# Seven-product down projection: unit widths, two sets of raw weights, and who adds the helping sum

## The chip, the core and the metric

The kernel runs on one core of a Trainium2 chip. Its engines run side by side, each through its own queue in order, and meet at semaphores: TensorE (PE; its weight loads are PEld), VectorE (DVE), ScalarE (ACT), GpSimd (POOL) and SyncE (SP), which here only issues DMAs. The metric is the device time of one execution in microseconds.

## The reference

Two layers of a bidirectional encoder over 1024 positions and width 1024, in float32: latent attention, then a gated MLP, differential attention, then another gated MLP, with a norm before each sub-layer and one at the end. The change touches the second half of the MLP alone:

```python
def conv_ffn(h, w_up, conv_w, conv_b, w_down):
    u = h @ w_up                       # 1024 -> 2 * 2816
    u = depthwise_conv3(u) + conv_b    # over positions
    g, val = jnp.split(u, 2, axis=-1)
    return (jax.nn.silu(g) * val) @ w_down   # 2816 -> 1024
...
    x = x + conv_ffn(rmsnorm(x, ffn_norm_g[i]), ...)
```

## The kernel before

Each float32 matmul is made of three passes over operands split in a high and a low part (`passes`): high by high, high by low, low by high. A split is a copy to the high part on ScalarE and a subtraction for the low part, on GpSimd for weights and on VectorE for activations.

Both MLP matmuls use a fast scheme with seven products instead of eight (Strassen's, in Winograd's form). For the down projection, weights and activations y are cut in 2 x 2 blocks; seven products of sums of blocks (0 to 6, in the order of `DOWN_A`: A11, S2, A12, S1, S4, S3, A22) give the four quarters of the output. S1 to S4 are sums of raw weight blocks, which GpSimd makes (`sum_a`). The sums of y blocks (T1 to T4) are made while the up projection runs, and stored in DRAM with the blocks; SP loads them back (`load_y`), and the weights (`load_a`: the even half holds A11 and A21, the odd half A12 and A22).

The inner width of 2816 is cut in 11 pairs. `SUPER` joins them in units: unit 0 is one pair wide, units 1 to 5 two. A unit runs its seven products, so there are 42 steps. One product makes four banks of PSUM (i = 0 to 3), with 12 matmuls a pair. VectorE adds each bank to a total in SBUF (`add_product`), four instructions a product. Products 0 and 1 go into `common`, a helping sum that three quarters of the output need; product 3 goes into `fifth`, which two need; 2, 4, 5 and 6 go straight into the output `x_out`, which already holds x. Products 2 and 6 continue in the banks of products 0 and 5, so product 6 waits until product 5 has been added, bank by bank. After the last `fifth` product VectorE adds `common` to `fifth` (L1363) and both to the output (L1346), between the last products' adds.

The order is that of the code. VectorE runs `low_y(step + 4)`, the split of a y block four steps ahead, before `add_product(step)`. ScalarE runs `high(g, n)` for each step in turn: the high part of the weight block, then that of the y block. GpSimd runs, for each unit, S1, S2, low A11, S4, low S2, low A12, low S1, S3, low S4, low S3, low A22; `sum_a` writes the raw sum over the low part of the unit before, so it waits for that product. There is one set of raw weights, and SP (`fetch`) asks for the next unit's even half when the sum S3 and the low parts are made.

At the start of the projection the up projection of the last pair still ends: its product with A22 (`fourth`), VectorE's `finish`, convolution and y sums. At the end ScalarE squares the output, GpSimd sums the squares (L1205, L1208) and TensorE adds over partitions (L1479), for the next norm; in layer 0 GpSimd first splits two weights of the next phase (L360).

## Time and profile before

| what | value |
|---|---|
| median of 3 runs (lowest, highest) | 2931.86 us (2930.26, 2936.58) |
| profiled execution, its span | 2930.89 us, 2929.0 us |
| busy PE, DVE, ACT, POOL | 93%, 69%, 49%, 55% |
| down projection of layer 0 (to the square sums) | 1182.3 to 1464.7 us |
| down projection of layer 1 | 2632.3 to 2908.1 us |

A row of a timeline has the start in us from the span's start, the duration, the engine, the line, the operation, what it writes and reads, and how many such instructions in a row were merged. In brackets stand the idle time before it and what ended that. Matmuls are pipelined, so that rows of PE overlap: the time from start to start is what a matmul costs. Instructions of the other engines also overlap by some 0.08 us.

### The profile page before, as it was taken

The page shows a single profiled execution, that of the slowest core. Times are in us where ns is not written, and L with a number is a line of the kernel's source. Part 1 is how long each engine was busy: PE and PEld are TensorE (multiplying, and loading weights), DVE is VectorE, ACT ScalarE, POOL GpSimd, SP SyncE. Part 2 cuts the span into 40 slices and gives each one's busy share as a digit, 9 for nine tenths or more (in the row PEclk, how much of TensorE's full clock was granted, in tenths as well). Part 3 has the DMA queues.
Part 4 walks back from the last instruction along what each step waited for, and adds up shares of the span by engine and source line. Part 5 has one row for each costly group of instructions (what it writes and reads, how often), then busy time and mean ns, then how long its engine had stood idle before and what let it go on. Part 6 is the DMA issues. An engine that isn't in the chain of part 4 may idle for free. (4 is left out here: it accounts for less than half of the span.)

```text
span 2929.0 us, 40309 instructions
## 1 busy us (share of the span) xinstructions
PE 2712.9 (93%) x13444; PEld 2274.4 (78%) x13444; DVE 2023.4 (69%) x2669; ACT 1421.3 (49%) x2182; POOL 1612.6 (55%) x1163
## 2 busy tenths in 40 slices
PE   8899999989899999699789999998898999997997
PEld 6788888878778888577678888887786888875775
DVE  6577777762766666677778888887428666667777
ACT  5577777761444444332345666665324444433332
POOL 2355554543787776576743333331237777765774
PEclk9999999999999999799999999999999999997998
DMA  3000000013132222544120010000331222225431
GB/s 134 22 11 10 7 10 7 15 64 114 36 116 106 98 99 107 201 138 137 43 110 22 30 37 29 31 20 22 151 110 43 106 94 107 107 104 204 145 130 65
DMA packets 90590, 230.00 MB, mean 79 GB/s; under 512 B 8944, under 2 KB 12272, under 8 KB 89968
## 3 DMA queue, kind: packets, MB, share of 16 engines
q1 hardware_dynamic: 90480, 228.57, 21.4%
q8 instruction: 65, 1.06, 0.1%
q14 instruction: 45, 0.37, 0.0%
HBM read 166.14 MB, written 62.39 MB: 78 GB/s over the span
## 5 line engine op out<-in xcount | busy, mean ns | idle before, releaser
L1377 PE MATMUL ffn_ps<-ffn_b_hi,weights_hi 128*128 128x512 f32 x704 | 277.8, 395 | 21.0 <-POOL weights_lo L720 12.2
L1379 PE MATMUL ffn_ps<-ffn_b_hi,weights_lo 128*128 128x512 f32 x704 | 276.7, 393 | 0.0
L1378 PE MATMUL ffn_ps<-ffn_b_lo,weights_hi 128*128 128x512 f32 x704 | 276.5, 393 | 0.0
L360 POOL TENSOR_TENSOR weights_lo<-weights_raw,weights_hi 128x1024 fp32r<-128x1024 f32 (+2 forms) x65 | 127.5, 1966 | 207.1 <-ACT weights_hi L355 207.1
L720 POOL TENSOR_TENSOR up_local_lo<-up_sums,up_local_hi 128x512 fp32r<-128x512 f32 x126 | 170.8, 1358 | 98.2 <-ACT up_local_hi L715 98.2
L2482 ACT ACTIVATE dif_p<-dif_s,dif_neg_max 128x1024 f32<-128x1024 f32 x128 | 142.2, 1114 | 121.9 <-DVE dif_neg_max L2669 115.5
L1377 PE MATMUL ffn_ps<-ffn_b_hi,up_local_hi 128*128 128x512 f32 x504 | 196.6, 390 | 0.0
L1378 PE MATMUL ffn_ps<-ffn_b_lo,up_local_hi 128*128 128x512 f32 x504 | 196.4, 390 | 0.0
L1379 PE MATMUL ffn_ps<-ffn_b_hi,up_local_lo 128*128 128x512 f32 x504 | 196.1, 389 | 0.0
L2572 POOL TENSOR_TENSOR dif_q_lo<-dif_rotated,dif_q_hi 64x512 fp32r<-64x512 f32 x64 | 85.1, 1330 | 182.5 <-ACT dif_q_hi L2464 178.8
L715 ACT ACTIVATE up_local_hi<-up_sums 128x512 fp32r<-128x512 f32 x126 | 79.0, 631 | 216.4 <-PE ffn_ps L1379 153.4
L2034 DVE TENSOR_REDUCE mat_row_max<-lat_s 128x1 f32<-128x1024 f32 x128 | 156.1, 1220 | 39.1 <-PE lat_s L371 38.1
L1887 ACT ACTIVATE mat_pt_hi<-mat_turn 128x512 fp32r<-128x512 f32 x256 | 138.9, 594 | 85.3 <-PE mat_turn L2160 85.0
L1377 PEld LDWEIGHTS ffn_ps<-ffn_b_hi,weights_hi 128*128 128x128 f32 x704 | 133.9, 190 | 52.7 <-issue 17.9
L1979 POOL TENSOR_TENSOR mat_passed<-mat_inv_sum 128x1 f32<-128x1 f32 x128 | 24.7, 193 | 264.2 <-DVE mat_inv_sum L2042 264.1
L1237 DVE SCALAR_TENSOR_TENSOR ffn_conv<-ffn_ps,vecs,ffn_conv 128x1023 f32<-128x1023 f32 x88 | 112.5, 1278 | 81.7 <-ACT ffn_conv L1035 81.7
L2669 DVE TENSOR_REDUCE dif_neg_max<-dif_s 128x1 f32<-128x1024 f32 x128 | 150.3, 1215 | 23.6 <-PE dif_s L2785 23.6
L2049 DVE TENSOR_TENSOR mat_pt_lo<-mat_turn,mat_pt_hi 128x512 fp32r<-128x512 f32 x256 | 162.8, 677 | 5.0 <-ACT mat_pt_hi L1887 5.0
L1115 ACT ACTIVATE ffn_hi_S<-ffn_raw_S 128x1024 fp32r<-128x1024 f32 (+1 forms) x48 | 47.1, 982 | 242.3 <-POOL ffn_raw_S L1176 242.3
L1907 ACT ACTIVATE mat_probs<-lat_s,mat_shift 128x1024 f32<-128x1024 f32 x128 | 143.5, 1121 | 25.6 <-DVE mat_shift L2037 25.3
L1378 PEld LDWEIGHTS ffn_ps<-ffn_b_lo,weights_hi 128*128 128x128 f32 x704 | 133.9, 190 | 27.8
L1379 PEld LDWEIGHTS ffn_ps<-ffn_b_hi,weights_lo 128*128 128x128 f32 x704 | 133.6, 190 | 28.1
(381 smaller groups left out, 8861.7 us busy)
## 6 DMA issues: line engine op xcount, KB each, us to landing
ffn_y_raw<-ffn_products SPq DMA_DIRECT2D x50, 512.0 KB, 3.5
weights_raw<-in_up SPq DMA_DIRECT2D x44, 512.0 KB, 3.3
up_raw<-in_up SPq DMA_DIRECT2D x44, 512.0 KB, 3.9
ffn_products<-ffn_y_sum SPq DMA_DIRECT2D x88, 256.0 KB, 2.2
ffn_a_raw<-in_down SPq DMA_DIRECT2D x44, 512.0 KB, 5.5
weights_raw<-in_diff_qkv SPq DMA_DIRECT2D x23, 512.0 KB, 3.2
ffn_products<-ffn_conv SPq DMA_DIRECT2D x44, 256.0 KB, 2.1
weights_raw<-ffn_products SPq DMA_DIRECT2D x20, 512.0 KB, 5.0
```

The source lines that it names most:

```text
L360: pool.tensor_tensor(w.lo[:], w.raw[:], w.hi[:].bitcast(F32), ALU.subtract).then_inc(w.lo_done, 1)
L720: pool.tensor_tensor(w.lo[name], w.block_raw(par, name), w.hi[name].bitcast(F32), ALU.subtract).then_inc(w.lo_done, 1)
L1237: dve.scalar_tensor_tensor(cv[:, 1:SEQ], pr[:, 0:SEQ - 1], vec(V_CONV_W + 2 * FT * 3 * layer, s, q), cv[:, 1:SEQ], ALU.mult, ALU.add).then ...
L1377: pe.matmul(out, hi, x_hi, start=start, stop=False, skip_group_check=True)
L1378: pe.matmul(out, hi, x_lo, start=False, stop=False, skip_group_check=True)
L1379: return pe.matmul(out, lo, x_hi, start=False, stop=stop, skip_group_check=True)
L1887: act.activation(pt[:, 4 * half:4 * half + 4, (t % 2) * P:(t % 2 + 1) * P], turn_ps[half][:].rearrange("p (k m) -> p k m", m=P), ACT.Copy) ...
L1907: act.activation(probs[t % 4][:], s_ps[t % 2][:], ACT.Exp, bias=shift[:, col:col + 1], scale=MLA_SCALE, accum_out=row_sum[:, col:col + 1]) ...
L2034: dve.tensor_reduce(row_max[:, col:col + 1], s_ps[t % 2][:], AX_X, ALU.max, negate=True).then_inc(max_ready, 1)
L2049: dve.tensor_tensor(pt_lo[b][part], turn_ps[half][:].rearrange("p (k m) -> p k m", m=P), pt_hi[b][part].bitcast(F32), ALU.subtract).then_i ...
L2482: act.activation((p0, p1)[m][t % 2][:], s_ps[m][:], ACT.Exp, bias=neg_max[:, col:col + 1], accum_out=total).then_inc(exp_done, 1)
L2669: dve.tensor_reduce(neg_max[:, col:col + 1], s_ps[m][:], AX_X, ALU.max, negate=True).then_inc(max_ready, 1)
```

## The change

The units are now (0, 1), (2, 3), ..., (8, 9), and 10 alone: the single pair stands last. There are two sets of raw weights (`even0`, `odd0`, `even1`, `odd1`), used in turn; the low part of A12, which lies on its raw block, has two places too. The raw sums S1 to S4 still have one place each. SP asks for both halves of a unit's weights first in `fetch`, and for y blocks 0 and 1 of unit 0 behind its weights, before the last stores of the up projection. `fourth` now runs between banks 1 and 2 of the first product. The adds of `common` to the output move from VectorE to GpSimd, 12 instructions in the place of VectorE's 8 (it no longer goes by way of `fifth`), and VectorE's early order changes. Both MLP layers run the same code.

```diff
 DOWN_SUMS = ("S1", "S2", "S4", "S3")
 Y_ROW = {B11: 0, T2: 1, B21: 2, T1: 3, B22: 4, T3: 5, T4: 6}
-SUPER = [(0, 1)] + [(2 * g - 1, 2) for g in range(1, 6)]
+SUPER = [(2 * g, 2) for g in range(5)] + [(10, 1)]
 STEPS = 7 * len(SUPER)
 COMMON, LAST_COMMON = (0, 1, 3), STEPS - 4
 DOWN_FINAL = [(k, 0, STEPS - 5) for k in range(4)] + [(k, 1, STEPS - 3) for k in range(4)] + \
@@ -733,7 +733,12 @@
 
 def added(step, i):
 
-    return 4 * step + i + 1 + (12 if step > LAST_COMMON else 0) + (4 if step > LAST_COMMON + 1 else 0)
+    return 4 * step + i + 1 + (4 if step > LAST_COMMON else 0) + (4 if step > LAST_COMMON + 1 else 0)
+
+
+def loaded(g):
+
+    return 16 * sum(width for first, width in SUPER[:g + 1])
 
 
 def stored(q, even):
...
-        self.a_raw = {"A11": ar[:, 0], "A21": ar[:, 1], "A12": ar[:, 2], "A22": ar[:, 3]}
+        self.even = [kb(f"even{b}", place, F32, (2, 2, 4, P)) for b, place in enumerate((124, 112))]
+        self.odd = [kb(f"odd{b}", place, F32, (2, 2, 4, P)) for b, place in enumerate((132, 176))]
+        self.a_own = [{"A11": even[:, 0], "A21": even[:, 1], "A12": odd[:, 0], "A22": odd[:, 1]}
...
@@ -948,7 +962,7 @@
 
             def load_a(g, odd):
                 first, width = SUPER[g]
-                tile, done = (down.odd, odd_loaded) if odd else (down.even, even_loaded)
+                tile, done = (down.odd[g % 2], odd_loaded) if odd else (down.even[g % 2], even_loaded)
                 for j in range(width):
                     sp.dma_start(tile[:, :, j], down_dram[2 * (first + j) + odd].rearrange("p (a k) m -> p a k m", a=2)) \
                       .then_inc(done, 16)
@@ -965,6 +979,9 @@
...
                     load_a(0, 1)
+                    sp.wait_ge(lo_done, block_no(PAIRS - 2, "A22"))
+                    load_y(0, 0)
+                    load_y(0, 1)
                 elif not (isinstance(p, int) and p == PAIRS - 2):
                     sp.wait_ge(lo_done, block_no(p, "A22"))
                     load_raw(p + 2, par)
...
 
-            sp.wait_ge(lo_done, block_no(PAIRS - 2, "A22"))
-            load_y(0, 0)
-            load_y(0, 1)
             sp.wait_ge(prod, product_no(PAIRS - 1, "P1"))
             load_y(0, 2)
             sp.wait_ge(prod, product_no(PAIRS - 1, "P6"))
...
             store_y(PAIRS - 1, False)
 
             def fetch(g):
+                if g == 1:
+                    sp.wait_ge(y_stored, 112 * GROUPS)
+                else:
+                    sp.wait_ge(a_summed, 4 * g - 4)
+                    sp.wait_ge(a_lo_done, 7 * g - 7)
+                    multiplied(sp, 7 * g - 12)
+                load_a(g, 0)
+                load_a(g, 1)
                 for n in range(2):
                     sp.wait_ge(y_lo_done, 7 * g - 7 + n + 1)
                     load_y(g, n)
-                sp.wait_ge(a_summed, 4 * g)
-                sp.wait_ge(a_lo_done, 7 * g - 6)
-                load_a(g, 0)
-                multiplied(sp, 7 * g - 5)
-                load_y(g, 2)
-                sp.wait_ge(a_lo_done, 7 * g)
-                load_a(g, 1)
-                for n in range(3, 7):
+                for n in range(2, 7):
                     multiplied(sp, 7 * g - 7 + n)
                     load_y(g, n)
 
...
             def sum_a(g, name, first, second, op, loads, sums):
-                width, raw_a = SUPER[g][1], down.a_raw
+                width = SUPER[g][1]
                 for done in loads:
-                    pool.wait_ge(done, 32 * g + 16 * width - (16 if g else 0))
+                    pool.wait_ge(done, loaded(g))
                 need(pool, a_summed, 4 * g + sums)
                 multiplied(pool, 7 * g - 7 + DOWN_A.index(name))
...
                 low_a(g, "S3")
                 low_a(g, "A22")
+            for n in (4, 5, 6):
+                for i in range(4):
+                    pool.wait_ge(acc_added, added(LAST_COMMON - 2, i))
+                    pool.tensor_tensor(x_part(n, i), x_part(n, i), down.common[:, i, :], ALU.add).then_inc(common_added, 1)
             if ahead:
                 ahead.split_low(pool)
             for n, (k, half, step) in enumerate(DOWN_FINAL[:-1]):
...
                     ins.then_inc(acc_added, 1)
 
-            def shared(n, i):
-
-                return added(LAST_COMMON, 3) + {6: 4, 4: 8, 5: 16}[n] + i + 1
-
-            def add_common(n):
+            def add_fifth(n):
                 for i in range(4):
-                    if n != 6:
-                        dve.wait_ge(acc_added, added(LAST_COMMON, 3) + i + 1)
-                    dve.tensor_tensor(x_part(n, i), x_part(n, i), (down.common if n == 6 else down.fifth)[:, i, :],
-                                      ALU.add).then_inc(acc_added, 1)
+                    dve.wait_ge(acc_added, added(LAST_COMMON, i))
+                    dve.wait_ge(common_added, 4 * (n - 4) + i + 1)
+                    dve.tensor_tensor(x_part(n, i), x_part(n, i), down.fifth[:, i, :], ALU.add).then_inc(acc_added, 1)
 
             low_y(0)
             low_y(1)
             finish(PAIRS - 1, 1)
             add_product(0)
+            low_y(2)
             finish_y(PAIRS - 1, False)
             sum_y(PAIRS - 1, False)
-            low_y(2)
             low_y(3)
+            add_product(1)
             low_y(4)
-            for step in range(1, LAST_COMMON + 1):
+            low_y(5)
+            for step in range(2, LAST_COMMON + 1):
                 low_y(step + 4)
                 add_product(step)
-            for i in range(4):
-                dve.wait_ge(acc_added, added(LAST_COMMON, i))
-                dve.tensor_tensor(down.fifth[:, i, :], down.fifth[:, i, :], down.common[:, i, :],
-                                  ALU.add).then_inc(acc_added, 1)
-            add_common(6)
-            add_common(4)
+            add_fifth(4)
             add_product(STEPS - 3)
-            add_common(5)
+            add_fifth(5)
             add_product(STEPS - 2)
             add_product(STEPS - 1)
             norm_mean(dve, out_norm)
...
                 for i in range(4):
+                    if between and i == 2:
+                        between()
                     if g == 0 and not more and i in (0, 2) and n in (0, 1):
                         if n == 0 and i == 2:
                             pe.wait_ge(u2_done, PAIRS - 1)
...
+            multiply_down(0, lambda: fourth(PAIRS - 1))
             for step in range(1, STEPS):
                 multiply_down(step)
             parts = ((out_norm.acc, 1, 0, out_norm.sq_added, 12), (out_norm.acc, 0, 0, out_norm.sq_added, 15),
```

VectorE in the last unit of layer 0, from the add of its product 2 on. Before (`ffn_ps` is PSUM, `x_first` the output):

```order
L1335 TENSOR_TENSOR x_first<-x_first,ffn_ps 128x512 x4
L1335 TENSOR_TENSOR ffn_fifth<-ffn_fifth,ffn_ps 128x512 x4
L1363 TENSOR_TENSOR ffn_fifth<-ffn_fifth,ffn_common 128x512 x4
L1346 TENSOR_TENSOR x_first<-x_first,ffn_common 128x512 x4
L1346 TENSOR_TENSOR x_first<-x_first,ffn_fifth 128x512 x4
L1335 TENSOR_TENSOR x_first<-x_first,ffn_ps 128x512 x4
L1346 TENSOR_TENSOR x_first<-x_first,ffn_fifth 128x512 x4
L1335 TENSOR_TENSOR x_first<-x_first,ffn_ps 128x512 x8
```

After the change:

```order
L1352 TENSOR_TENSOR x_first<-x_first,ffn_ps 128x512 x4
L1352 TENSOR_TENSOR ffn_fifth<-ffn_fifth,ffn_ps 128x512 x4
L1359 TENSOR_TENSOR x_first<-x_first,ffn_fifth 128x512 x4
L1352 TENSOR_TENSOR x_first<-x_first,ffn_ps 128x512 x4
L1359 TENSOR_TENSOR x_first<-x_first,ffn_fifth 128x512 x4
L1352 TENSOR_TENSOR x_first<-x_first,ffn_ps 128x512 x8
L212 TENSOR_SCALAR diff_norm_stat<-ffn_ps 128x8
```

The row of L1363 and one of the two kinds of L1346 are gone. The adds of products 5 and 6 (x8 before, and x8 now) stand last in both.

GpSimd at the same place, before the change:

```order
L1176 TENSOR_TENSOR ffn_raw_S_5393<-ffn_a_raw 128x1024
L1182 TENSOR_TENSOR ffn_lo_S_5405<-ffn_raw_S_5392,ffn_hi_S_5398 128x1024
L1182 TENSOR_TENSOR ffn_lo_S_5406<-ffn_raw_S_5393,ffn_hi_S_5399 128x1024
L1182 TENSOR_TENSOR ffn_lo_A_5407<-ffn_a_raw,ffn_hi_A_5400 128x1024
L360 TENSOR_TENSOR weights_lo<-weights_raw,weights_hi 128x1024 x2
L1205 COPY ffn_sq<-ffn_sq 128x512
L1208 TENSOR_TENSOR ffn_sq<-ffn_sq 128x512 x3
L1205 COPY ffn_sq<-ffn_sq 128x512
```

And after it:

```order
L1191 TENSOR_TENSOR ffn_raw_S_5396<-ffn_even_5390 128x512
L1197 TENSOR_TENSOR ffn_lo_S_5407<-ffn_raw_S_5395,ffn_hi_S_5401 128x512
L1197 TENSOR_TENSOR ffn_lo_S_5408<-ffn_raw_S_5396,ffn_hi_S_5402 128x512
L1197 TENSOR_TENSOR ffn_lo_A_5409<-ffn_odd_5392,ffn_hi_A_5403 128x512
L1217 TENSOR_TENSOR x_first<-x_first,ffn_common 128x512 x12
L360 TENSOR_TENSOR weights_lo<-weights_raw,weights_hi 128x1024 x2
L1224 COPY ffn_sq<-ffn_sq 128x512
L1227 TENSOR_TENSOR ffn_sq<-ffn_sq 128x512 x3
```

The 12 helping adds (L1217) stand between the last low parts and the next phase's weight splits, and the square sums come behind both. The blocks of the last unit are half as wide.

SP, in the fetching of a unit (`ffn_even`, `ffn_odd` are raw weights; `weights_raw` is the place of y blocks 0 and 1). Before the change:

```order
L946 DMA weights_raw<-ffn_products 128x2x512 x2
L953 DMA ffn_a_raw<-in_down 128x2x512 x2
L946 DMA ffn_y_raw_5408<-ffn_products 128x2x512
L953 DMA ffn_a_raw<-in_down 128x2x512 x2
L946 DMA ffn_y_raw_5409<-ffn_products 128x2x512
L946 DMA ffn_y_raw_5410<-ffn_products 128x2x512
L946 DMA ffn_y_raw_5411<-ffn_products 128x2x512
L946 DMA ffn_y_raw_5412<-ffn_products 128x2x512
```

And after it:

```order
L967 DMA ffn_even_5390<-in_down 128x2x512 x2
L967 DMA ffn_odd_5392<-in_down 128x2x512 x2
L960 DMA weights_raw<-ffn_products 128x2x512 x2
L960 DMA ffn_y_raw_5412<-ffn_products 128x2x512
L960 DMA ffn_y_raw_5413<-ffn_products 128x2x512
L960 DMA ffn_y_raw_5414<-ffn_products 128x2x512
L960 DMA ffn_y_raw_5415<-ffn_products 128x2x512
L960 DMA ffn_y_raw_5416<-ffn_products 128x2x512
```

The four weight loads stood on both sides of y block 2, behind y blocks 0 and 1; now they are first.

## Rows read from the trace of the kernel before

**Rows 1.** Windows: stretch, length; busy PE, PEld, DVE, ACT, POOL; clock; DMA.
```profile
1182.30:1239.20 56.90, 32.21 (x97) 24.51 (x98) 38.19 (x46) 20.13 (x26) 27.50 (x14) 0.70 0.61 227
1239.20:1409.10 169.90, 157.33 (x673) 128.68 (x672) 124.29 (x142) 54.50 (x56) 124.57 (x45) 0.97 0.41 137
1409.10:1464.70 55.60, 40.86 (x179) 33.44 (x177) 46.45 (x51) 16.97 (x24) 37.93 (x22) 0.90 0.09 29
2632.30:2690.10 57.80, 32.33 (x98) 24.43 (x98) 37.90 (x46) 20.13 (x26) 27.29 (x14) 0.70 0.60 223
2690.10:2857.40 167.30, 154.87 (x666) 126.66 (x665) 126.71 (x142) 54.51 (x56) 124.78 (x45) 0.98 0.41 139
2857.40:2908.10 50.70, 42.72 (x186) 34.95 (x184) 39.09 (x51) 15.30 (x22) 31.57 (x20) 0.93 0.04 11
```

**Rows 2.** Timeline of PE, rows with idle time before them, layer 0.
```profile
1186.11 0.77 PE L1377 MATMUL ffn_ps<-ffn_y_hi,ffn_hi_A 128*128 128x512 f32 x1 [3.86 <-DVE weights_lo L1310]
...
1234.16 0.77 PE L1377 MATMUL ffn_ps<-ffn_y_hi,ffn_hi_A 128*128 128x512 f32 x1 [7.77 <-DVE x_first L1335]
...
1274.87 0.47 PE L1377 MATMUL ffn_ps<-ffn_y_hi,ffn_hi_A 128*128 128x512 f32 x1 [2.90 <-DVE x_first L1335]
...
1454.21 0.77 PE L1377 MATMUL ffn_ps<-ffn_y_hi,ffn_hi_A 128*128 128x512 f32 x1 [12.24 <-DVE x_first L1335]
```

**Rows 3.** Timeline of PE, first and last matmul of product 3, unit 1.
```profile
1255.49 0.39 PE L1377 MATMUL ffn_ps<-ffn_y_hi,ffn_hi_S 128*128 128x512 f32 x1
...
1260.70 0.39 PE L1379 MATMUL ffn_ps<-ffn_y_hi,ffn_lo_S 128*128 128x512 f32 x1
```

**Rows 4.** Timelines of SP, ACT, DVE in the start, and one group by form.
```profile
1166.83 1.33 SPq L953 DMA_DIRECT2D ffn_a_raw<-in_down  x2
...
1182.05 0.88 SPq L946 DMA_DIRECT2D weights_raw<-ffn_products  x2
...
1184.61 0.63 ACT L1117 ACTIVATE ffn_y_hi<-weights_raw 128x512 fp32r<-128x512 f32 x1 [10.75 <-DMA weights_raw<-ffn_products]
...
1217.82 1.06 ACT L1115 ACTIVATE ffn_hi_A<-ffn_a_raw 128x1024 fp32r<-128x1024 f32 x1 [15.05 <-DMA ffn_a_raw<-in_down]
...
1247.09 3.41 DVE L1310 TENSOR_TENSOR ffn_y_lo<-ffn_y_raw,ffn_y_hi 128x1024 fp32r<-128x1024 f32 x1
...
L1310 DVE TENSOR_TENSOR ffn_y_lo<-ffn_y_raw,weights_hi 128x1024 fp32r<-128x1024 f32 x5 | 6.1, 1211 | 0.0
```

**Rows 5.** Timelines of POOL and DVE, middle, late in unit 1.
```profile
1262.30 2.39 POOL L1176 TENSOR_TENSOR ffn_raw_S<-ffn_a_raw 128x1024 f32<-128x1024 f32 x1 [9.52 <-DMA ffn_a_raw<-in_down]
...
1274.05 2.47 DVE L1335 TENSOR_TENSOR x_first<-x_first,ffn_ps 128x512 f32<-128x512 f32 x4
```

**Rows 6.** Timeline of DVE in the end, layers 0 and 1.
```profile
1431.73 6.89 DVE L1363 TENSOR_TENSOR ffn_fifth<-ffn_fifth,ffn_common 128x512 f32<-128x512 f32 x4
...
1447.95 5.51 DVE L1346 TENSOR_TENSOR x_first<-x_first,ffn_fifth 128x512 f32<-128x512 f32 x4
...
2884.14 2.49 DVE L1346 TENSOR_TENSOR x_second<-x_second,ffn_common 128x512 f32<-128x512 f32 x4
```

**Rows 7.** Timeline of POOL, both layers, and one group by form.
```profile
1176.12 2.33 POOL L1182 TENSOR_TENSOR ffn_lo_A<-ffn_a_raw,ffn_hi_A 128x512 fp32r<-128x512 f32 x1
...
1430.15 5.21 POOL L360 TENSOR_TENSOR weights_lo<-weights_raw,weights_hi 128x1024 fp32r<-128x1024 f32 x2 [7.88 <-ACT weights_hi L355]
...
1447.72 4.60 POOL L1208 TENSOR_TENSOR ffn_sq<-ffn_sq 128x512 f32<-128x512 f32 x3
...
2890.36 0.61 POOL L1205 COPY ffn_sq<-ffn_sq 128x512 f32<-128x512 f32 x1 [11.80 <-ACT ffn_sq L1134]
...
2891.11 4.61 POOL L1208 TENSOR_TENSOR ffn_sq<-ffn_sq 128x512 f32<-128x512 f32 x3
...
2898.22 9.83 POOL L1208 TENSOR_TENSOR ffn_sq<-ffn_sq 128x512 f32<-128x512 f32 x7 [2.49 <-ACT ffn_sq L1134]
...
L1176 POOL TENSOR_TENSOR ffn_raw_S<-ffn_a_raw 128x512 f32<-128x512 f32 x1 | 1.3, 1291 | 0.0
```

More of the change, by code:

```diff
@@ L1170, in sum_a @@
             def sum_a(g, name, first, second, op, loads, sums):
[L1171 removed]
+                width = SUPER[g][1]
                 for done in loads:
[L1173 removed]
+                    pool.wait_ge(done, loaded(g))
                 need(pool, a_summed, 4 * g + sums)
                 multiplied(pool, 7 * g - 7 + DOWN_A.index(name))
[L1176 to L1177 removed]
+                pool.tensor_tensor(down.raw_of(g, name)[:, 0:width], down.raw_of(g, first)[:, 0:width],
+                                   down.raw_of(g, second)[:, 0:width], op).then_inc(a_summed, 1)
             def low_a(g, name):
@@ L1181, in low_a @@
                 pool.wait_ge(a_hi_done, 7 * g + DOWN_A.index(name) + 1)
-                pool.tensor_tensor(down.a_lo[name][:, 0:width], down.a_raw[name][:, 0:width],
+                pool.tensor_tensor(down.lo_of(g, name)[:, 0:width], down.raw_of(g, name)[:, 0:width],
                                    down.a_hi[name][:, 0:width].bitcast(F32), ALU.subtract).then_inc(a_lo_done, 1)
```

35 lines of the change are left out of this document (18 added, 17 removed).

## The prediction

> **What bounds the kernel now.** I read the page first: TensorE is busy 93% of the span, and in its row of tenths the two down projections stand out (slice 17 is a 6; 20, 37 and 40 are 7). Next the windows, cut at three points of each down projection [rows 1]: from the end of the last up product to the end of down unit 0 (the start), from there through units 1 to 4 (the middle), and from the first product of unit 5 to the sums of squares on TensorE (the end). A matmul of 128x512 goes out every 0.2265 us at full clock (first and last of the 24 of one product, 1255.49 and 1260.70 [rows 3]), so a product of a two-wide unit takes 5.44 us, a two-wide unit of seven 38.1, a one-wide unit 19.05, and the left-over up product "fourth" 2.72. Against that the stretches lose: start 56.9 - 21.8 = 35.1 (second layer 57.8: 36.0), middle 169.9 - 152.3 = 17.6 (167.3: 15.0), end 55.6 - 38.1 = 17.5 (50.7: 12.6). Together 133.8 us in which the matrix engine waits or runs at 1.2 instead of 2.4 GHz (the granted clock is 0.70 in the start). The projections are bound by its waits, and the number of matmuls does not change.
>
> Then the rows of TensorE with idle time before them [rows 2]. The start waits 3.86 us for the first split y block (ScalarE waits for its DMA, 10.75 us [rows 4]), and 7.77 us before product 6 of unit 0: VectorE's adding of product 5 is queued behind a split for unit 1 whose raw weights were asked for late; ScalarE idles 15.05 us for them [rows 4]. Every following unit waits before product 6, 2.90 us in the one shown, 2.8 to 3.9 in all eight of both layers. The end waits 12.24 for the same add, which stands behind the twelve and more sums of the helping totals.
>
> **The start.** Removed: the late request (y blocks 0 and 1 were asked for at 1182.05; they now stand behind the weight loads of 1166.83 to 1168.16 [rows 4], some 13 us earlier), the one-wide first unit, and the one set of raw weights. Added: the first unit is twice as wide, so its splits and sums double in width on GpSimd, ScalarE and VectorE, and the loads double in size; the x loads stand in the same place. TensorE has 40.8 us of work there (38.1 + 2.72) instead of 21.8 for the same VectorE tail of the up projection, which is cover. I walked VectorE's queue forward from its last y sum, which ended just before TensorE ran dry at 1182.3 [rows 1]. A split of 128x1024 takes it 1.21 alone or 3.41 when it meets GpSimd [rows 4]; four product adds take 2.4 from start to start (2.47 with the end of the last [rows 5]). With the splits that meet GpSimd at 3.4, TensorE waits about 1.6 us for y block 0, 1 for the up product's add, 3.2 before product 3 (finish_y and three sums precede the adds of product 1), 3.4 before product 4 (splits 4, 5 and 6 precede the adds of product 2), 2 before product 6, and about 3 at half clock after the two longer waits: 14. With all at 1.21 the same walk leaves 2; with nine splits each 2.2 dearer, 22. I take 13, near the walk with collisions, since GpSimd works through doubled blocks all the while. Saved: 35.1 - 13 = 22.1 and 36.0 - 13 = 23.0. The fourth product between bank halves costs nothing: the add it needs is that 1 us late; without this cover it would wait for the 2.7 us of the add and its convolution.
>
> **The middle.** With two sets the loads are out a unit ahead, so GpSimd's first sum no longer waits for DMA. But it still writes the single S1 tile, whose low part product 3 of the unit before reads. Product 3 ended at 1260.70 + 0.39 = 1261.09 and the sum began at 1262.30 [rows 3, 5], so 1.1 to 1.2 us can be saved. From that start the chain runs unchanged, through the S2 sum, ScalarE's splits, VectorE's split, the adds of product 4 and the first of product 5 at 1274.05 [rows 5], to TensorE's 1274.87 [rows 2]: 12.57 us. Product 6 could issue at 1260.70 + 0.23 + 48 x 0.2267 = 1271.8 and did 3.1 late. Now it is 1261.2 + 12.6 = 1273.8, 2.0 late. That holds before product 6 of units 1, 2 and 3, each of which prepares a two-wide unit: 3 x 1.96 = 5.9. Unit 4 prepares a one-wide unit, with the chain's pieces halved (some 8 us), and does not wait. The rest of the old loss, 5.4 and 2.8, is half clock after longer waits; I keep 2.9. New middle 8.8: saved 8.8 and 6.2. The bounds of the 5.9 are 0 and the old 12.2.
>
> **The end.** Counted from E, the first product of the one-wide unit 5. VectorE is nearly full: it has 2.4 for each product's adds, and a split beside them, against TensorE's 2.72. So adds of product 0 end at about E+4.3, of 1 at +7.3 (the first at +5.6), of 2 at +11.3, of 3 at +13.7. GpSimd has its last low part by +2.2, and waits for that first add at +5.6. Its 12 sums: alone 1.29 each, 1.53 in the group that met VectorE (4.60 for three; 1.38 in the mean here) [rows 7]: 16.6, to +22.2. VectorE's sums of two SBUF operands take 2.49 for four when GpSimd is idle and 5.51 when it works, 6.89 against two wide ones [rows 6]. I take 5.5 twice: fifth into product 4's part to +19.2, adds of 4 to +21.6, fifth into 5's to +27.1, first add of 5 to +27.8. TensorE could issue product 6 at +16.3 and now does at +27.8, at half clock after such a wait (12 x 0.45 = 5.4); VectorE ends near +34. That is the old wait in another place, though eight VectorE sums are gone.
>
> Behind the 12 sums stand GpSimd's 15 square sums: 5.36 for a copy and three, twice, and 9.83 for the last seven [rows 7], 20.55. So the sums of squares reach TensorE at +22.2 + 20.6 = +42.8, 23.8 after the work of 19.05. In layer 0 two splits of the next phase's weights (5.2 [rows 7]) stand between: 29.1. Against 12.6 and 17.5 the end loses 11.2 and 11.6. The helper adds formerly lay in VectorE's idle time only in part; now GpSimd's queue is the path. Bounds: all GpSimd work undisturbed, 12 x 1.29 and 18.0 for the squares, gives 20.0; each of 27 operations at 2.33, the dearest row of a 128x512 one [rows 7], gives 49.5.
>
> A rule of the Trainium skill weighs here. SBUF — State Buffer, "Who interferes with whom", says that a VectorE instruction with both inputs in SBUF and a GpSimd one that reads SBUF exclude each other for a whole instruction. The 5.51 is less than strict alternation, 4 x (0.60 + 1.29) = 7.6. By the rule GpSimd would also be held 8 x 0.6: about 3.4 us more in each end, and a time of some 2901.
>
> **The sum.** Start -45.1, middle -15.0, end +22.8: -37.3 us. The profiled execution took 2930.89 (span 2929.0 and 1.9 around it), giving 2893.6; the median of the three runs, 2931.86, is 1.0 above it. I forecast 2894.
>
> **Rivals.** Short splits: VectorE's splits seldom meet GpSimd, the start loses 2 instead of 13. For it: half the splits in the middle take 1.21; against it: three in a row at 3.4 whenever GpSimd splits. 2894 - 22 = 2872. Two sets free the middle wholly: the 5.9 goes to 0 in both layers. Against it stands the wait for product 3 on the S1 tile. 2882. Start stays long: nine dear splits, doubled y loads behind 4 MB of x; start loses 22: 2894 + 18 = 2912. The queue of GpSimd, on the other side: the 12 sums and 15 squares at 2.33 each because VectorE holds it off, in the one-wide last unit where nothing covers them; the end loses 49.5 and 54.8, 25.7 more each: 2945. It decides from about 2.1 us an operation, where (2.1 - 1.39) x 27 = 19 eats up half the sum in each layer. For it: one such row of 2.33; against it: 4.60 for three beside VectorE's own dense sums. That the change does not do what it says (loads no earlier) would show as the second layer's start above 30; it is contained in the long start.
>
> **How the numbers follow.** Forecast 0.55, short splits 0.15, free middle 0.12, long start 0.13, GpSimd queue 0.05. Range 2872 to 2914: from the short splits to just past the long start; under 2 in 10 lies outside. A measurement of this kernel can tell 0.2%, 5.9 us, from no change. Faster 0.93, same 0.02, slower 0.05.
>
> **What would show it.** Right: TensorE's wait before product 6 near 1.8 us in units 1 to 3 and none in 4; before product 6 of unit 5 near 10 us with VectorE as releaser; GpSimd without a pause from the first helping sum to the last square, some 37 us (42 in layer 0); start stretches near 54 us. Wrong: a start over 62 or under 45, an end under 38 us, or helping sums over 2 us each.

## The result, and the profile after

| what | before | after |
|---|---|---|
| median of 5 runs (lowest, highest) | 2931.86 us (2930.26, 2936.58) | 2918.33 us (2913.00, 2922.69) |
| ratio after to before, 95% interval | | 0.9949 (0.9932 to 0.9965) |
| profiled execution, its span | 2930.89 us, 2929.0 us | 2922.69 us, 2920.8 us |

The change makes the kernel faster by 13.5 us, not by the 38 of the forecast, and the time lies above the range of 2872 to 2914. The whole interval of the ratio is under 1, so that the gain is real, though it is only 0.5%. The windows of the kernel after, cut at the same places as [rows 1] (columns: stretch, length; busy PE, PEld, DVE, ACT, POOL; granted clock; DMA share, GB/s):

```profile
1185.03:1248.60 63.57, 45.51 (x182) 35.76 (x182) 53.80 (x48) 24.05 (x25) 45.87 (x16) 0.92 0.59 215
1248.60:1408.94 160.34, 154.70 (x673) 127.02 (x672) 123.58 (x140) 51.87 (x58) 118.45 (x48) 0.99 0.38 128
1408.94:1457.34 48.40, 23.22 (x94) 18.66 (x92) 33.88 (x40) 14.45 (x22) 43.04 (x30) 0.74 0.08 27
2627.96:2694.50 66.54, 49.93 (x181) 39.27 (x181) 54.70 (x49) 24.77 (x25) 47.75 (x17) 0.82 0.56 206
2694.50:2856.47 161.97, 156.32 (x674) 128.17 (x672) 120.37 (x140) 51.98 (x58) 117.07 (x47) 0.98 0.38 127
2856.47:2899.91 43.44, 22.80 (x94) 18.35 (x92) 31.10 (x40) 12.66 (x20) 38.09 (x28) 0.77 0.02 7
```

The widths have moved 19.05 us of bare TensorE work from the end to the start, so a stretch is to be read against its bare work (40.8, 152.3 and 19.05 us now). What it has over that, layer 0 and layer 1:

| over the bare work, us | before [rows 1] | forecast | after |
|---|---|---|---|
| start | 35.1, 36.0 | 13, 13 | 22.8, 25.7 |
| middle | 17.6, 15.0 | 8.8, 8.8 | 8.0, 9.7 |
| end | 17.5, 12.6 | 29.1, 23.8 | 29.4, 24.4 |

Against before the start gives 22.6, the middle 14.9, and the end takes 23.6: 13.9 us gained, which is the difference of the medians. The span of the profiled execution fell by only 8.2, since the rest of the program took 5.7 more in it. That is chance: the same kernel run again had a span of 2916.1 with 2369.2 outside of these stretches, against 2370.8 before and 2376.5 here; over all the kernels below this part varies from 2367 to 2378.

TensorE's rows with idle time, which answer to [rows 2] (timeline of PE of the kernel after):

```profile
1188.22 0.47 PE L1386 MATMUL ffn_ps<-ffn_y_hi,ffn_hi_A 128*128 128x512 f32 x1 [3.03 <-DVE weights_lo L1329]
...
1217.46 0.76 PE L1386 MATMUL ffn_ps<-ffn_y_hi,ffn_hi_S 128*128 128x512 f32 x1 [7.53 <-DVE ffn_common L1352]
1218.02 0.63 PE L1387 MATMUL ffn_ps<-ffn_y_lo,ffn_hi_S 128*128 128x512 f32 x1
...
1232.38 0.47 PE L1386 MATMUL ffn_ps<-ffn_y_hi,ffn_hi_S 128*128 128x512 f32 x1 [2.19 <-DVE ffn_fifth L1343]
...
1241.59 0.77 PE L1386 MATMUL ffn_ps<-ffn_y_hi,ffn_hi_A 128*128 128x512 f32 x1 [3.49 <-DVE x_first L1352]
...
1283.28 0.47 PE L1386 MATMUL ffn_ps<-ffn_y_hi,ffn_hi_A 128*128 128x512 f32 x1 [1.88 <-DVE x_first L1352]
...
1438.63 0.76 PE L1386 MATMUL ffn_ps<-ffn_y_hi,ffn_hi_A 128*128 128x512 f32 x1 [13.21 <-DVE x_first L1352]
1453.12 1.87 PE L1489 MATMUL ffn_ps<-ones,ffn_sq 128*128 128x1 f32 x8 [9.62 <-POOL ffn_sq L1227]
```

From the top: the first product, then product 3, 5 and 6 of unit 0; product 6 of unit 1 (2.90 before, and 1.88 in units 1, 2 and 3 alike now, none in unit 4); product 6 of unit 5; the sums of squares. The new large wait is the 7.53 before product 3, 7.54 in layer 1. After it matmuls go out 0.43 us apart, at half clock. Its releaser is VectorE's add of product 1. What VectorE did before that add, and GpSimd beside it (timelines of DVE and POOL of the kernel after):

```profile
1203.86 3.41 DVE L1284 TENSOR_TENSOR ffn_conv<-ffn_conv 128x1024 f32<-128x1024 f32 x1
1207.30 2.78 DVE L1294 TENSOR_TENSOR ffn_y_sum<-ffn_conv,ffn_y_sum 128x512 f32<-128x512 f32 x1
1210.01 2.82 DVE L1295 TENSOR_TENSOR ffn_y_sum<-ffn_conv,ffn_y_even 128x512 f32<-128x512 f32 x1
1212.75 2.82 DVE L1297 TENSOR_TENSOR ffn_y_sum<-ffn_conv,ffn_y_sum 128x512 f32<-128x512 f32 x1
...
1202.80 3.39 POOL L1191 TENSOR_TENSOR ffn_raw_S<-ffn_even 128x1024 f32<-128x1024 f32 x1
1206.15 6.13 POOL L1197 TENSOR_TENSOR ffn_lo_S<-ffn_raw_S,ffn_hi_S 128x1024 fp32r<-128x1024 f32 x2
1212.24 2.79 POOL L1197 TENSOR_TENSOR ffn_lo_A<-ffn_odd,ffn_hi_A 128x1024 fp32r<-128x1024 f32 x1
1228.08 2.39 POOL L1191 TENSOR_TENSOR ffn_raw_S<-ffn_even,ffn_odd 128x1024 f32<-128x1024 f32 x1 [13.05 <-DMA ffn_odd<-in_down]
```

`finish_y` and the three y sums, all with both operands in SBUF, take 11.8 us. GpSimd works without a pause through its four last instructions of unit 0, 12.2 us for what takes 2.4 each alone. The two engines take turns here: each VectorE instruction of 512 columns (0.6 alone) lasts about as long as itself and one GpSimd instruction of 1024. SP stores these y sums and asks for unit 1's weights only behind the stores (timelines of SP and ACT of the kernel after), so that GpSimd (13.05, above) and ScalarE stand idle and unit 0's products 5 and 6 come late as well:

```profile
1215.61 1.31 SPq L941 DMA_DIRECT2D ffn_products<-ffn_y_sum  x3
1218.94 1.21 SPq L967 DMA_DIRECT2D ffn_even<-in_down  x2
...
1225.46 1.06 ACT L1130 ACTIVATE ffn_hi_A<-ffn_even 128x1024 fp32r<-128x1024 f32 x1 [15.27 <-DMA ffn_even<-in_down]
```

The end went as forecast, 48.4 and 43.4 us, with GpSimd busy from the first helping sum to the last square (timelines of DVE and POOL of the kernel after; compare [rows 6, 7]):

```profile
1421.90 5.83 DVE L1359 TENSOR_TENSOR x_first<-x_first,ffn_fifth 128x512 f32<-128x512 f32 x4
...
1430.05 7.84 DVE L1359 TENSOR_TENSOR x_first<-x_first,ffn_fifth 128x512 f32<-128x512 f32 x4
...
1414.10 17.75 POOL L1217 TENSOR_TENSOR x_first<-x_first,ffn_common 128x512 f32<-128x512 f32 x12 [2.52 <-DVE ffn_common L1352]
1431.81 5.53 POOL L360 TENSOR_TENSOR weights_lo<-weights_raw,weights_hi 128x1024 fp32r<-128x1024 f32 x2
...
1443.35 13.94 POOL L1227 TENSOR_TENSOR ffn_sq<-ffn_sq 128x512 f32<-128x512 f32 x10
```

### The profile page after: what moved, and what is told of

Its sections match the earlier page's. It is cut to its first block and busy times, and to the rows that moved or that the text cites. A ratio compares the mean times of both kernels' runs of the same rounds, so it can differ in the third digit from the quotient of the medians.

```text
span 2920.8 us, 40331 instructions
## 1 busy us (share of the span) xinstructions
PE 2715.0 (93%) x13444; PEld 2277.9 (78%) x13444; DVE 2025.1 (69%) x2653; ACT 1423.1 (49%) x2182; POOL 1645.2 (56%) x1187
## 5 line engine op out<-in xcount | busy, mean ns | idle before, releaser
L1386 PE MATMUL ffn_ps<-ffn_y_hi,ffn_hi_S 128*128 128x512 f32 x352 | 139.2, 395 | 18.0 <-DVE ffn_common L1352 15.1
```

Of the source, the lines that this page charges most:

```text
L1386: pe.matmul(out, hi, x_hi, start=start, stop=False, skip_group_check=True)
```

## The experiments

All edits are against the kernel after. Two theories of the start stood against each other: the collision (the y sums are long because GpSimd's wide instructions hold them off), and the late data (the start is bound by loads or by the amount of work in front of product 3, and the y sums only fill the time). Stretches as above, layer 0 / layer 1:

| kernel | start | middle | end | median us | ratio to before (95%) |
|---|---|---|---|---|---|
| before | 56.9 / 57.8 | 169.9 / 167.3 | 55.6 / 50.7 | 2931.86 | 1 |
| after | 63.6 / 66.5 | 160.3 / 162.0 | 48.4 / 43.4 | 2918.33 | 0.9949 (0.9932 to 0.9965) |
| the same again | 66.1 / 64.9 | 162.0 / 162.0 | 48.4 / 43.4 | 2917.88 | 0.9943 (0.9925 to 0.9960) |
| hold | 54.7 / 55.8 | 162.0 / 160.4 | 48.4 / 43.4 | 2898.04 | 0.9884 (0.9865 to 0.9902) |
| reorder | 65.4 / 64.5 | 160.3 / 162.0 | 48.4 / 43.4 | 2918.61 | 0.9959 (0.9942 to 0.9977) |
| halves | 60.0 / 63.0 | 160.4 / 162.0 | 48.4 / 43.4 | 2913.78 | 0.9948 (0.9932 to 0.9964) |
| swap | 65.5 / 64.7 | 152.3 / 152.3 | 48.9 / 43.9 | 2900.98 | 0.9889 (0.9870 to 0.9908) |
| helpback | 65.5 / 64.5 | 162.0 / 162.0 | 44.8 / 39.6 | 2913.86 | 0.9926 (0.9906 to 0.9946) |
| oneset | 65.8 / 65.8 | 165.5 / 161.0 | 48.4 / 43.4 | 2926.11 | 0.9975 (0.9962 to 0.9988) |
| units | 49.2 / 48.9 | 162.5 / 162.5 | 56.8 / 51.8 | 2904.76 | 0.9906 (0.9885 to 0.9927) |
| best | 52.4 / 52.8 | 152.3 / 152.3 | 45.4 / 40.2 | 2872.46 | 0.9794 (0.9772 to 0.9817) |
| besthalf | 48.0 / 50.2 | 152.6 / 152.6 | 47.1 / 40.2 | 2868.62 | 0.9789 (0.9771 to 0.9806) |
| bestold | 38.8 / 39.8 | 153.5 / 153.5 | 55.6 / 48.9 | 2863.66 | 0.9779 (0.9762 to 0.9796) |

units and bestold have the old widths, so their bare work is 21.8 in the start and 38.1 in the end. Each ratio is to runs of before beside it.

**The same kernel again.** No edit; it shows what moves by itself.

> The changed kernel once more, as the yardstick for the others of this call. Its first measurement was 2918.33 us, its profiled run 2922.69 us. In that trace the start takes 63.6 and 66.5 us, the middle 160.3 and 162.0, the end 48.4 and 43.4, and the rest of the program 5.9 us more than in the profile before. If those 5.9 us are chance, this trace shows the rest within 3 us of the kernel before; if the change causes them, again about 6 us more.

The same 2918, and a start differs by up to 2.5 us, by how many matmuls go out at half clock after the waits: the start of layer 0 takes 66.1 us at a granted clock of 0.82 here, and took 63.6 at 0.92 in the first profile. (Layer 1 of the first profile has eleven of them after the first wait, of 3.78, and again after the one of 7.54; granted clock 0.82.)

**hold.** GpSimd's fourth sum of unit 0 waits until the y sums are done.

```diff
                 low_a(g, "S1")
+                if g == 0:
+                    pool.wait_ge(y_summed, 2 * PAIRS)
                 sum_a(g, "S3", ...)
```

> GpSimd waits, in down unit 0 only, until VectorE has made the last y sums, before it makes the raw sum S3 and the low parts of S4, S3 and A22. Theory (collision): the 7.53 us before product 3 come from four y instructions of VectorE (3.41, 2.78, 2.82, 2.82 us) that each wait for a GpSimd instruction of 1024 columns; alone they took 0.6 to 1.8. Then the y sums end some 6 us sooner, product 3 waits under 2 us, and the loads of unit 1, which stand behind the stores of these sums, come 6 us sooner, so that product 6 waits less too: start about 54 and 57 us, time about 2918 - 19 = 2899. Rival (order): the adds of product 1 stand behind finish_y and three sums whatever these cost, and the halved work of GpSimd comes too late for products 4 and 5: start within 3 us of 63.6 and 66.5, time 2912 to 2924.

Timelines of DVE, POOL and PE of hold:

```profile
1203.52 1.21 DVE L1286 TENSOR_TENSOR ffn_conv<-ffn_conv 128x1024 f32<-128x1024 f32 x1
1204.77 0.69 DVE L1296 TENSOR_TENSOR ffn_y_sum<-ffn_conv,ffn_y_sum 128x512 f32<-128x512 f32 x1
1205.38 0.68 DVE L1297 TENSOR_TENSOR ffn_y_sum<-ffn_conv,ffn_y_even 128x512 f32<-128x512 f32 x1
...
1210.11 10.01 DVE L1331 TENSOR_TENSOR ffn_y_lo<-ffn_y_raw,ffn_y_hi 128x1024 fp32r<-128x1024 f32 x3
...
1206.75 3.32 POOL L1191 TENSOR_TENSOR ffn_raw_S<-ffn_even 128x1024 f32<-128x1024 f32 x1 [4.23 <-DVE ffn_y_sum L1299]
...
1220.87 0.77 PE L1388 MATMUL ffn_ps<-ffn_y_hi,ffn_hi_S 128*128 128x512 f32 x1 [5.85 <-DVE x_first L1354]
```

The four instructions take 3.3 us instead of 11.8, the waits before products 3, 5 and 6 are gone, and the kernel gains 20 us although GpSimd stood still for 4.2 us. The instructions, their operands and their place in VectorE's order are the same; only what GpSimd does meanwhile differs. That is the collision. A part of it moves on: splits 4, 5 and 6 now meet GpSimd's work (10.01 for three, 3.34 each) and product 4 waits 5.85.

**reorder.** The adds of product 1 are put ahead of `finish_y` and the y sums.

```diff
             low_y(2)
+            low_y(3)
+            add_product(1)
             finish_y(PAIRS - 1, False)
             sum_y(PAIRS - 1, False)
-            low_y(3)
-            add_product(1)
```

> VectorE splits y block 3 and adds product 1 before finish_y and the three y sums, instead of after; GpSimd unchanged. Theory (collision): the sums still meet GpSimd's wide instructions and take some 11 us in place of 3, so the 7.5 us before product 3 go to product 4, and the stores and the loads of unit 1 come later, so product 6 waits longer: start 62 to 70 us, time 2915 to 2925. Rival (order): only the place of the adds made TensorE wait; product 3 starts at once, nothing takes its place, start about 57, time about 2903.

Timelines of DVE and PE of reorder:

```profile
1205.10 3.40 DVE L1284 TENSOR_TENSOR ffn_conv<-ffn_conv 128x1024 f32<-128x1024 f32 x1
1208.53 2.76 DVE L1294 TENSOR_TENSOR ffn_y_sum<-ffn_conv,ffn_y_sum 128x512 f32<-128x512 f32 x1
1211.22 0.68 DVE L1295 TENSOR_TENSOR ffn_y_sum<-ffn_conv,ffn_y_even 128x512 f32<-128x512 f32 x1
...
1216.65 0.77 PE L1386 MATMUL ffn_ps<-ffn_y_hi,ffn_hi_S 128*128 128x512 f32 x1 [5.78 <-DVE x_first L1352]
```

The wait leaves product 3 and stands before product 4 (5.78) and product 5 (4.08, and 4.98 in layer 1); the time does not move. The four y instructions did not take the 11 us expected but 7.5: the split of y block 3, now ahead of them, took its turn beside GpSimd instead (3.40, against 1.21 in the change), and the last two y sums came when GpSimd had run out of work (0.68 each). So moving the adds alone gains nothing while VectorE and GpSimd collide; that the order counts too is seen in best, where the 5.85 before product 4 of hold is gone.

**halves.** GpSimd's sums and low parts of unit 0 are each issued as two instructions of 512 columns.

```diff
-                pool.tensor_tensor(lo[:, 0:width], raw[:, 0:width], hi[:, 0:width], ALU.subtract).then_inc(a_lo_done, 1)
+                for part in ([slice(j, j + 1) for j in range(width)] if g == 0 else [slice(0, width)]):
+                    ins = pool.tensor_tensor(lo[:, part], raw[:, part], hi[:, part], ALU.subtract)
+                ins.then_inc(a_lo_done, 1)
```

(and `sum_a` likewise; names shortened here)

> The change, with each of GpSimd's eleven instructions of unit 0 cut into two of half the width (512 columns instead of 1024); order and waits stay. Theory (collision by length): a VectorE instruction waits for the one GpSimd instruction under way, so each of the four y instructions costs its own 0.6 to 1.2 plus at most 1.3, not 2.4: together 7 to 8 us instead of 11.8; the wait before product 3 falls from 7.5 to 3 to 5, the start to 59 to 62 us, the time to about 2910. Rival (shared rate): both engines are slowed in proportion to the work that lies together, which is the same; the y instructions take 11 to 12 us again and the time is within 4 us of 2918.

Timelines of DVE, POOL and PE of halves:

```profile
1209.83 1.66 DVE L1298 TENSOR_TENSOR ffn_y_sum<-ffn_conv,ffn_y_sum 128x512 f32<-128x512 f32 x1
...
1206.44 4.50 POOL L1192 TENSOR_TENSOR ffn_raw_S<-ffn_even 128x512 f32<-128x512 f32 x2
1210.90 7.31 POOL L1200 TENSOR_TENSOR ffn_lo_S<-ffn_raw_S,ffn_hi_S 128x512 fp32r<-128x512 f32 x4
...
1191.20 0.77 PE L1390 MATMUL ffn_ps<-ffn_y_hi,ffn_hi_A 128*128 128x512 f32 x1 [5.09 <-POOL ffn_lo_A L1200]
...
1217.83 0.47 PE L1390 MATMUL ffn_ps<-ffn_y_hi,ffn_hi_S 128*128 128x512 f32 x1 [4.28 <-DVE ffn_common L1356]
```

GpSimd has the same columns to do and VectorE the same sums, yet a sum takes 1.7 us instead of 2.8, all four y instructions 7.5 instead of 11.8, and the wait before product 3 falls from 7.53 to 4.28. What VectorE pays here is one GpSimd instruction, of whatever length that has; the rival of a rate that both engines share falls. The time gains nothing that these runs can tell: 4.6 us by the medians, but the ratios to before are 0.9948 and 0.9949 (the two starts are 7 us shorter in the profiles). Now GpSimd gives way more often, low A11 is late, and the first product waits 5.09 for it.

**swap.** From step 7 on VectorE adds a product before it splits a y block for four steps ahead.

```diff
             for step in range(2, LAST_COMMON + 1):
-                low_y(step + 4)
-                add_product(step)
+                if step < 7:
+                    low_y(step + 4)
+                    add_product(step)
+                else:
+                    add_product(step)
+                    low_y(step + 4)
```

> From step 7 on VectorE adds the product of a step before it splits the y block of four steps later, instead of after. Theory (chain): the 1.88 us before product 6 in units 1 to 3 come from VectorE's queue, where the split of block 1 of the next unit, which waits for GpSimd's sums S1 and S2, stands ahead of the adds of products 4 and 5. Then this wait is gone (below 0.5 us) and the middle is 154 to 157 us instead of 160.3 and 162.0: about 10 us less, 2908. Rival (load): VectorE is simply late with its own work, and splits held by GpSimd push the adds anyway: the waits stay at 1.5 to 2 us, or move to another product, and the time is within 3 us of 2918.

Windows of the middle of both layers in swap (columns as in the first fence):

```profile
1247.98:1400.30 152.32, 152.32 (x674) 126.13 (x673) 117.59 (x139) 51.60 (x58) 118.02 (x47) 1.00 0.40 135
2681.98:2834.30 152.32, 152.32 (x673) 126.13 (x672) 116.40 (x139) 51.60 (x58) 120.20 (x48) 1.00 0.39 135
```

TensorE does not wait once in 152.3 us, and the clock is at full speed throughout. The last link of the forecast's chain (the S sum, the high parts, VectorE's split, then the adds of products 4 and 5) was right: it was the order of split and adds on VectorE. The gain, 17 us, is more than the 11.3 of the waits (6 of 1.88), because the half-clock matmuls behind some of them go too; the 8.0 and 9.7 over the bare work go whole.

**helpback.** VectorE adds the helping sum, as before the change.

```diff
-            for n in (4, 5, 6):    # GpSimd, 4 instructions each
-                ... pool.tensor_tensor(x_part(n, i), x_part(n, i), down.common[:, i, :], ALU.add)
...
-            add_fifth(4)
+            (fifth += common: 4 instructions)
+            add_common(6)
+            add_common(4)
             add_product(STEPS - 3)
-            add_fifth(5)
+            add_common(5)
```

(lines with `...` or words in the place of code are shortened; the waits in `add_product` and `added` go back to those of before too)

> Everything of the change but the helping sum, which VectorE adds again as before (through fifth), so that GpSimd's 12 adds are gone. Theory (queue): in the one-wide last unit GpSimd's queue of 12 adds (17.8 us) and 15 square sums sets the end, and without the adds VectorE's chain to product 6 of 29 us after the start of the unit sets it, with the last squares some 8 us behind: end about 38 us in both layers instead of 48.4 and 43.4, time about 2918 - 15 = 2903. Rival: VectorE's extra 12 sums cost it more than the adds of GpSimd do, product 6 starts 5 us later than now and the end grows: 2918 + 5 to 10.

Timelines of DVE, POOL and PE of helpback:

```profile
1426.39 2.50 DVE L1357 TENSOR_TENSOR x_first<-x_first,ffn_common 128x512 f32<-128x512 f32 x4
...
1433.60 7.10 DVE L1357 TENSOR_TENSOR x_first<-x_first,ffn_fifth 128x512 f32<-128x512 f32 x4
...
1425.58 10.22 POOL L360 TENSOR_TENSOR weights_lo<-weights_raw,weights_hi 128x1024 fp32r<-128x1024 f32 x2 [11.13 <-ACT weights_hi L355]
...
1442.53 13.99 POOL L1223 TENSOR_TENSOR ffn_sq<-ffn_sq 128x512 f32<-128x512 f32 x10
...
1452.36 1.87 PE L1493 MATMUL ffn_ps<-ones,ffn_sq 128*128 128x1 f32 x8 [6.04 <-POOL ffn_sq L1223]
```

The end is 3.6 and 3.8 us shorter in the profile, so handing the sum to GpSimd costs rather than helps here; the size was overestimated (38 us expected, 44.8 and 39.6 measured), and by the medians it is 4.5 us, with intervals of the ratios that overlap. VectorE's first twelve sums take 2.50 for four although GpSimd has a weight split under way: this time GpSimd bears it, and its first split takes 7.92 us (10.22 for both, against 5.53 in the change). Only the last group of sums pays itself, beside the second split and the first squares (7.10). Product 6 starts 29.7 us after unit 5 begins in layer 0 of both kernels (29.2 in layer 1, against 26.9 with the change): up to there VectorE gains nothing, or only 2.3 us, by giving the sum away, since its fewer instructions are longer. What GpSimd's 17.75 us cost comes later, in the squares: TensorE's wait for them falls from 9.62 to 6.04, and in layer 1 from 7.86 to 1.27.

**oneset.** One set of raw weights, with the loads in the old places.

```diff
-        self.raw_of = lambda g, name: self.a_own[g % 2][name] ...
+        self.raw_of = lambda g, name: self.a_own[0][name] ...
-                tile, done = (down.odd[g % 2], odd_loaded) if odd else (down.even[g % 2], even_loaded)
+                tile, done = (down.odd[0], odd_loaded) if odd else (down.even[0], even_loaded)
```

(and the low part of A12 in one place, and `fetch` as before the change)

> The change with one set of raw weights and the order of loads that goes with it. Theory (chain): before product 6 of units 1 to 3 the wait is again 2.9 to 3.1 us instead of 1.88, 1.2 us each, and the start loses a few us, since the weights of unit 1 wait for the low part of A22 of unit 0: 2918 + 8 to 16. Rival (the second set is worth nothing, since S1 and S2 have one place): the waits stay at 1.9 and the time within 3 us of 2918.

```profile
1242.55 0.77 PE L1385 MATMUL ffn_ps<-ffn_y_hi,ffn_hi_A 128*128 128x512 f32 x1 [6.75 <-DVE x_first L1351]
...
1286.69 0.77 PE L1385 MATMUL ffn_ps<-ffn_y_hi,ffn_hi_A 128*128 128x512 f32 x1 [3.17 <-DVE x_first L1351]
```

(timeline of PE of oneset: product 6 of units 0 and 1.) These waits were 3.49 and 1.88 with two sets; in the other units they are 2.5 to 2.7 now, where 2.9 to 3.1 were expected. By the medians the second set is worth 8 us (2926.1 against 2918). The stretches of the profiled execution show 3 to 6 of them, and the rest may be chance.

**units.** The old widths, the single pair first, with all else of the change.

```diff
-SUPER = [(2 * g, 2) for g in range(5)] + [(10, 1)]
+SUPER = [(0, 1)] + [(2 * g - 1, 2) for g in range(1, 6)]
```

> The change with the old unit widths: unit 0 one pair, the others two; two sets, early y loads and the helping sum on GpSimd stay. Theory (widths move the loss to the end): the one-wide unit at the end leaves GpSimd's 27 adds uncovered (end 48.4 and 43.4 us for 19.05 of work, 29 and 24 over); under a two-wide last unit the same queue costs 8 to 12 over (end 46 to 50), while the start, whose bare work is then 21.8, is about 30 over (52 us). Together some 10 us a layer less: 2898. Rival (the wide first unit pays): the start loses the cover of the up projection's tail and is again 35 over (57 us) and the end gains less than 10 us a layer: 2915 to 2925.

13 us faster than the change as it is: the two ends grow by 8.4 each, the starts are 14 to 18 shorter. The start has 27.4 and 27.1 over its bare 21.8, the end 18.7 and 13.7 over 38.1, where 8 to 12 were expected. So the new widths lose: over the bare work the start is only 1 to 5 us better with them, and the end 10.7 worse. A part of that is the collision again: with a narrow first unit GpSimd's instructions beside the y sums are half as wide, and the four y instructions take 5.3 us in layer 0 (2.30, 1.66, 0.68, 0.68) instead of 11.8.

**best.** hold, helpback and an order of VectorE with the adds first from the beginning, in the new widths.

```diff
             add_product(1)
             low_y(4)
-            low_y(5)
             for step in range(2, LAST_COMMON + 1):
-                low_y(step + 4)
                 add_product(step)
+                if step <= 7:
+                    low_y(step + 3)
+                if step >= 7:
+                    low_y(step + 4)
```

(beside the edits of hold and helpback)

> Four edits together: GpSimd holds in unit 0 until the y sums are made; VectorE adds before it splits from step 2 on, with splits three steps ahead until step 7 and four from then on; the helping sum is VectorE's again. Theory: the parts add up. Start: 54.7 less the 5.85 before product 4, about 48; middle bare, 152.3; end 44.8 and 39.6. With 2372 us outside and 1.9 around the span: 2859. Rival (the waits trade places): VectorE's work in the start cannot be moved without a wait for a split elsewhere, start stays at 54 or more: 2871 or more.

Middles bare, ends as in helpback, but the start came to 52.4 and 52.8, not 48: the first wait (3.37 and 3.78) and one of 3.29 before product 6 stay. The median missed what was expected (2859) by 13 us, 9 of them in the starts, and lies at the time of the rival in which the waits trade places, though its starts of 54 did not come; it is still 46 below the change's.

**besthalf** (best with halves' edit) and **bestold** (best with the widths of units):

> The fastest version with GpSimd's unit 0 instructions cut in halves. Theory (collision by length): VectorE's splits of y blocks 0 and 1, which took 3.4 us each beside wide GpSimd instructions, take under 2.4, so the first wait of TensorE (3.4 and 3.8 us) and the 3.3 us before product 6 shrink: start 49 to 50 instead of 52.4 and 52.8, time about 2867. Rival: those waits come from the order of the loads and sums before it, start within 1 us of 52.5.

> The four edits of the fastest version (GpSimd holds in unit 0, adds before splits, helping sum on VectorE) with the old unit widths, one pair first. Theory: in the old widths the start was 49.2 and 48.9 us (27 over its bare 21.8) and the wide last unit hid part of the end; with the edits the start is about 45, the middle 152.3, and the end 50 to 52, since VectorE's late sums still come after the last wide products: 247 to 249 us a layer, within 4 us of 2872 either way. Rival (the widths still decide as in the plain change, where the old ones were 13 us faster): 2860.

besthalf takes the starts to 48.0 and 50.2 and gains 4 us on best by the medians, which the intervals of the ratios don't tell apart; the wait before product 6 is gone there, and a first wait of 3.79 and 5.10, for GpSimd's low A11, stays. Its end in layer 0 is 1.7 us longer than that of best, with the same instructions there (timelines of DVE and POOL of besthalf):

```profile
1398.73 6.85 DVE L1384 TENSOR_TENSOR ffn_fifth<-ffn_fifth,ffn_common 128x512 f32<-128x512 f32 x4
...
1399.63 5.39 POOL L360 TENSOR_TENSOR weights_lo<-weights_raw,weights_hi 128x1024 fp32r<-128x1024 f32 x2 [11.05 <-ACT weights_hi L355]
```

In best these four sums took 2.49 and the two splits 9.71. So the same pair of engines settled the same collision once at VectorE's cost and once at GpSimd's; no run shows what decides that. bestold is the fastest by its median, though its interval too overlaps with that of best; its window of the start of layer 0:

```profile
1183.04:1221.83 38.79, 26.09 (x98) 19.42 (x98) 30.33 (x44) 13.56 (x19) 17.86 (x10) 0.87 0.87 319
```

17.0 us over the bare work in the start, with the DMA engines at 0.87: a wait of 7.92 before product 6 of the short first unit remains. The start is 6 us shorter than expected and the end of layer 0 is 55.6 where 50 to 52 were. Its ratio of 0.9779 is 2.2% or 64 us under before, with the widths and the helping sum as they were: the two sets with the earlier loads and the early order, the hold of GpSimd, and VectorE's adds ahead of its splits bring it.

## Why the prediction was wrong

**Faster** was right and given 0.93; the size was wrong, and one step holds all of it: the start, where 45.1 us were to be saved and 22.6 were. With the measured starts (over by 22.8 and 25.7 instead of 13) the sum is -37.3 + 22.5 = -14.8, against -13.9 in the windows and -13.5 in the medians. The long start was a rival with 0.13, at 22 over and 2912: near the size, but it laid the loss on dear splits and late loads, not on the y sums. The forecast's own sign of being wrong, a start over 62 us, came in both layers.

**The step that failed.** "3.2 before product 3 (finish_y and three sums precede the adds of product 1)". The forecast gave the splits their price beside GpSimd, 3.41 [rows 4], but `finish_y` and the y sums, instructions of the same kind with two operands in SBUF, got no such price: 3.3 us undisturbed, 11.8 measured, and with them 7.53 and 7.54 of wait where 3.2 stood. Step by step in layer 0, forecast and measured: first block 1.6 and 3.03 (the splits of y blocks 0 and 1 both met GpSimd, 3.38 and 3.40); the up product's add 1 and 0.86; product 2 nothing and 0.96; product 3 3.2 and 7.53; product 4 3.4 and none (GpSimd had run dry when splits 4 to 6 came, and they took their 1.21 each); products 5 and 6 2 and 2.19 + 3.49, behind the late loads of unit 1; half clock 3 and about 4. hold shows that this is the error: with the y sums undisturbed its starts are 13.9 and 15.0 over, where 13 was forecast. That the totals lie so close is in part luck, since in hold nothing waits before product 3 and 5.85 us before product 4, where 3.2 and 3.4 were forecast. The forecast had a row for such sums beside GpSimd's wide instructions (6.89 for four [rows 6]) and a rule for it in hand, and used both in the end of the projection alone.

The Trainium skill says in SBUF — State Buffer, "Who interferes with whom", that such a VectorE instruction and a GpSimd instruction that reads SBUF exclude each other, and that the one that issues first holds the other off for its whole length. In the start the traces agree, to within a tenth, if the two engines take strict turns: a sum of 0.6 beside one of 2.4 makes 3.0 and beside one of 1.28 makes 1.9; measured 2.8 and 1.7. In the ends they agree less. Four sums beside GpSimd's 512-column ones took 5.83, where strict turns make 7.6, and GpSimd's twelve took 17.75, where the forecast's reading of the rule, 12 x 1.29 + 8 x 0.6, makes 20.3 (3.7 us over its 16.6, not 3.4). In helpback and best twelve VectorE sums in a row ran at their undisturbed 0.6 while a GpSimd split waited its 5 us. The forecast had weighed this rule only where GpSimd's instructions were short.

**The middle** was right: 1.88 before product 6 in units 1, 2 and 3 (forecast 1.96 for each of three), none in unit 4, 8.0 and 9.7 over where 8.8 was forecast. The head of the chain shows in the trace, GpSimd's first sum released by TensorE's product 3, and 12.59 us from there to product 6 (12.57 forecast); swap shows that its last link was the cause of the wait. Timeline of POOL of the kernel after, unit 1:

```profile
1270.69 2.40 POOL L1191 TENSOR_TENSOR ffn_raw_S<-ffn_even,ffn_odd 128x1024 f32<-128x1024 f32 x1 [10.49 <-PE ffn_ps L1388]
```

**The end** was right in sum and nearly in each part. GpSimd's 12 sums ran from +5.2 to +22.9 (forecast +5.6 to +22.2), the squares took 20.0 (forecast 20.55), stretches 48.4 and 43.4 (48.1 and 42.9). The sums of `fifth` took 5.83 and 7.84 in layer 0, not 5.5 twice, and the wait before product 6 13.21 and 10.42, where 11.5 was forecast; it did not decide the end, the queue of GpSimd did, as forecast. The rival of 2.33 an operation fell: 17.75 / 12 = 1.48.

**The other rivals.** The change does what it says: with one set the kernel is 8 us slower by the medians. Short splits fell: blocks 0 and 1 took 3.38 and 3.40. The rival of free middles fell at the S1 tile, as argued (the row above).

What stays open: what the first wait alone is worth (no run with the wide first unit took it away; halves and besthalf only changed what it waits for), and what decides which of the two engines pays for a collision.

## What to carry to other kernels

Price every VectorE instruction with two SBUF operands by what GpSimd runs beside it: up to itself plus the length of one GpSimd instruction, so making GpSimd's instructions wider makes VectorE's short ones dearer. GpSimd can pay instead, as in helpback, so carry both prices as bounds. Where VectorE is on the critical path, let GpSimd wait a few microseconds (20 us gained here); cutting its instructions shorter made the collisions cheaper, but gained nothing that the runs could tell, since GpSimd's own results came later. And before work is moved from one end of a stage to the other, walk both ends with the same prices: the new widths took 10.7 us more at the end and gave 1 to 5 at the start.
